# Key masks ahead of the next chunk's decays, map transposes between two halves, and a join whose gaps hold other work

## The reference, cut to what matters

```python
def step(S, inp):
    r_t, w_t, k_t, v_t, a_t, b_t = inp
    sa = jnp.einsum('bhij,bhj->bhi', S, a_t)
    S = S * w_t[:, :, None, :] + sa[..., None] * b_t[:, :, None, :] + v_t[..., None] * k_t[:, :, None, :]
    y = jnp.einsum('bhij,bhj->bhi', S, r_t) if emit else None
    return S, y
```

```python
xn = rms_norm_2(h, attn_norm_g[layer])
proj = xn @ w_in[layer]
```

## Time and profile before

| what | value |
|---|---|
| runs | 1196.22, 1204.70, 1204.64 us; median 1204.64 |
| profiled execution | 1197.72 us (span 1195.9 us) |
| TensorE | 1131.4 us busy (95%), mean granted clock 0.972 |
| VectorE, ScalarE, GpSimd busy | 645.7, 337.4, 112.4 us |
| chain that ended last | PE 75%, DVE 17%, ACT 3%, DMA 2% |

### The profile page before, as it was taken

How to read it: one execution, slowest core, us unless ns; L and a number is a source line. 1 busy time by engine, 2 the same in 40 slices (tenths; PEclk the granted TensorE clock), 3 DMA queues, 4 the chain that set the end, 5 groups by cost and what they waited for, 6 DMA issues and landing times.

```text
span 1195.9 us, 15595 instructions
## 1 busy us (share of the span) xinstructions
PE 1131.4 (95%) x6191; PEld 787.1 (66%) x6191; DVE 645.7 (54%) x1360; ACT 337.4 (28%) x786; POOL 112.4 (9%) x107
## 2 busy tenths in 40 slices
PE   4899999979878999999999999999999999999997
PEld 2444857657778686556478888644555488888543
DVE  3222315766997965798226666631698135665400
ACT  2212223765643224225121121200525112112100
POOL 0000101110120011161000000100360000000000
PEclk9799999998888989999999999999999999999999
DMA  9722342000003202742248443434432354454410
GB/s 356 271 71 78 121 141 76 1 1 1 2 1 100 98 11 71 281 141 71 71 120 277 141 141 141 163 119 142 160 121 71 98 184 141 142 166 173 154 35 35
DMA packets 96666, 140.06 MB, mean 117 GB/s; under 512 B 12207, under 2 KB 63058, under 8 KB 96466
## 3 DMA queue, kind: packets, MB, share of 16 engines
q1 hardware_dynamic: 96228, 138.94, 34.2%
q10 hardware_dynamic: 366, 0.13, 0.0%
HBM read 138.01 MB, written 1.05 MB: 116 GB/s over the span
## 4 chain that ended last, share of the span: by engine, by line
PE 75%; DVE 17%; ACT 3%; DMA 2%; issue 2%; SPq 0%; POOL 0%; DVEq 0%; ACTq 0%
PE bank L1335 25%; PE bank L1354 13%; PE bank L825 12%; PE bank L480 2%; PE bank L473 2%; PE bank L1163 2%; DMA ring<-in_ada_w 2%; DVE work L2594 2%; DVE work L2589 1%; PE bank L1153 1%; PE bank L1044 1%; PE bank L1097 1%; PE bank L619 1%; DVE rot L2574 1%; DVE ring L2159 1%
## 5 line engine op out<-in xcount | busy, mean ns | idle before, releaser
L1335 PE MATMUL bank<-work,ring 128*128 128x256 f32 x1024 | 222.7, 379 | 0.0
L1335 PEld LDWEIGHTS bank<-work,ring 128*128 128x128 f32 x1024 | 194.2, 190 | 26.2
L825 PE MATMUL bank<-work,ring 128*128 128x256 f32 (+1 forms) x432 | 141.0, 485 | 2.4 <-ACT work L1405 2.4
L1354 PE MATMUL bank<-ring,work 128*128 128x512 f32 x288 | 124.2, 592 | 0.0
L825 PEld LDWEIGHTS bank<-work,ring 128*128 128x128 f32 x432 | 82.7, 194 | 56.0 <-issue 49.4
L1853 ACT ACTIVATE work<-work,prm 128x256 f32<-128x256 f32 x88 | 48.0, 593 | 250.5 <-DVE work L2734 224.0
L1354 PEld LDWEIGHTS bank<-ring,work 128*128 128x128 f32 x288 | 54.7, 190 | 68.0 <-issue 67.4
L2726 DVE TENSOR_TENSOR work<-bank,turned 128x512 f32<-128x512 f32 x44 | 30.4, 692 | 112.0 <-PE bank L1335 111.9
L1335 PE MATMUL bank<-work 128*128 128x256 f32 x384 | 83.9, 379 | 0.0
L1335 PEld LDWEIGHTS bank<-work 128*128 128x128 f32 x384 | 73.0, 190 | 9.9
L2744 DVE SCALAR_TENSOR_TENSOR work<-work,prm 128x256 f32<-128x256 f32 x176 | 77.1, 480 | 4.2 <-ACT work L1853 2.6
(11 more groups left out here) (454 smaller groups left out, 1759.7 us busy)
## 6 DMA issues: line engine op xcount, KB each, us to landing
ring<-in_w_up SPq DMA_DIRECT2D x32, 1024.0 KB, 7.7
ring<-in_w_in SPq DMA_DIRECT2D x24, 1024.0 KB, 7.7
ring<-in_w_down SPq DMA_DIRECT2D x16, 1024.0 KB, 6.0
ring<-in_ada_w SPq DMA_DIRECT2D x12, 1024.0 KB, 11.0
work<-in_w_up SPq DMA_DIRECT2D x12, 1024.0 KB, 7.7
ring<-in_w_out SPq DMA_DIRECT2D x10, 1024.0 KB, 6.2
work<-in_w_in SPq DMA_DIRECT2D x4, 1024.0 KB, 8.5
work<-in_w_down SPq DMA_DIRECT2D x4, 1024.0 KB, 6.0
```

Of the source, the lines that this page charges most:

```text
L825: ins = mm(b[0:rows, 0:toks], wt[:, k, off:off + rows], hT[:, k, 0:toks], start=(k == 0), stop=(k == KD - 1))
L1335: ins = mm(b[:, SEQ * half:SEQ * half + SEQ], wt[:, KD * half + k, P * j:P * j + P], xnT[:, k, :], start=(k == 0), stop=(k == KD - 1))
L1354: ins = mm(acc[2 * t + j][:, :], actT[:, k, P * t:P * t + P], wt[:, q, 512 * j:512 * j + 512], start=(k == 0), stop=(k == FB - 1))
```

## The change

The same instructions are issued, none is added or taken out (one semaphore, `row_inv`, is new). Five orders change:

1. `mask_tokens(n)` on VectorE comes ahead of `decayed(n+1)` and `rates(n+1)` in chunks 1 to 3 and 6, and between them in chunk 5. Chunks 4 and 7 stay.
2. In both joins ScalarE spreads the diagonals from the rows' result as soon as that exists (`row_inv`), copies `mid`, and spreads the others behind it.
3. In the second join one of the two bonus banks is filled behind `mid`, the other behind `corner`, and behind that the last matmul of the early projection; ScalarE copies that bank later. VectorE takes the bonus banks before `state_inputs`.
4. In both layers the small maps' transposes stand between `xa` 1 and `xa` 2.
5. ScalarE empties `xa` 0 before the last squares and `xa` 2 ahead of the maps; VectorE empties `xa` 1 before `wsT`.

```diff
@@ tensor: joins, early projection @@
                 ins.then_inc(*filling(("mid", p)))
                 if p:
-                    bonus_sums()
+                    bonus_sums(0)
                 pe.wait_ge(*when_empty(("mid", p)))
...
                 ins.then_inc(*filling(("corner", p)))
+                if p:
+                    bonus_sums(1)
...
-            project_early(0)
+            project_early(0, 0)
+            project_early(0, 1)
             advance(2)
             advance(3)
-            project_early(1)
+            project_early(1, 0)
+            project_early(1, 1, range(3))
+            join_quarters(1)
+            project_early(1, 1, range(3, 4))
             weights_done(("early", 1, 1))
-            join_quarters(1)
@@ tensor: seams @@
-                def to_channels(key, x, ready):
+                def to_channels(key, x, ready, between=None):
                     for j in range(4):
+                        if j == 2 and between:
+                            between()
                         if j % 2 == 0:
                             pe.wait_ge(*ready(j // 2))
...
-                    to_channels("xa", xc, lambda j: when_empty(("down", l - 1, 2 + j)))
+                    to_channels("xa", xc, lambda j: when_empty(("down", l - 1, 2 + j)), small_maps)
@@ scalar: joins @@
             def spread_quarters(p):
-                act.wait_ge(S["t_inv"], p + 1)
-                for d in range(2):
+                def diagonals(d):
+                    act.wait_ge(S[("row_inv", "t_inv")[d]], p + 1)
                     for q in range(2):
...
+                diagonals(0)
                 key = ("mid", p)
...
                 A.activation(mid, b[:, :], ACT.Copy).then_inc(*emptying(key))
+                diagonals(1)
...
             spread_quarters(1)
             state_parameters(0)
+            take_early(1, 1)
@@ scalar: seams @@
                 for t in range(2):
                     cols, q = slice(512 * j, 512 * j + 512), 2 * j + t
+                    if q == 3:
+                        channels_even(0, "xa", "attn_g", 0)
                     act.wait_ge(S["x1"], q + 1)
...
                     for q in range(4):
+                        if q == 2:
+                            channels_even(l, "xa", "attn_g", 0)
                         square_sum(2 * l, q, when_empty(("down", l - 1, 2 * (q % 2) + q // 2)))
+                channels_even(l, "xa", "attn_g", 2)
                 take_maps()
-                channels_even("xa", "attn_g", 0)
-                channels_even("xa", "attn_g", 2)
@@ vector @@
-                step(V.transpose(sq_c.rearrange("p (n x) -> p x n", n=32), t3))
+                V.transpose(sq_c.rearrange("p (n x) -> p x n", n=32), t3).then_inc(S["row_inv"], 1)
+                aside(next(passed))
...
             for n in range(1, 4):
+                mask_tokens(n)
                 decayed(n + 1)
                 rates(n + 1)
-                mask_tokens(n)
                 scaled(n + 1)
...
             for n in range(4, 8):
+                if n == 6:
+                    mask_tokens(n)
                 if n < 7:
                     decayed(n + 1)
+                    if n == 5:
+                        mask_tokens(n)
                     rates(n + 1)
-                mask_tokens(n)
+                if n in (4, 7):
+                    mask_tokens(n)
...
             join(1)
-            state_inputs(0)
             for j in range(2):
                 vec.wait_ge(*when_full(("bonus", j)))
...
+            state_inputs(0)
...
+                channels_odd("xa", "attn_g", (1,))
                 take_mixing()
-                channels_odd("xa", "attn_g")
+                channels_odd("xa", "attn_g", (3,))
```

More of the change, by code:

```diff
@@ L1037, in _, with project_early @@
             wt_a = weights("out_attention", 4, 1024)
-            def project_early(j):
-                for t in range(2):
+            def project_early(j, t, ks=range(4)):
+                if ks[0] == 0:
                     pe.wait_ge(*turn(("early", j, t)))
-                    b = bank_of(("early", j, t))
-                    for k in range(4):
-                        ins = mm(b[:, :], mixT[:, 4 + k, P * t:P * t + P], wt_a[:, k, 512 * j:512 * j + 512], start=(k == 0), stop=(k == 3))
+                b = bank_of(("early", j, t))
+                for k in ks:
+                    ins = mm(b[:, :], mixT[:, 4 + k, P * t:P * t + P], wt_a[:, k, 512 * j:512 * j + 512], start=(k == 0), stop=(k == 3))
+                if ks[-1] == 3:
                     ins.then_inc(*filling(("early", j, t)))
@@ L1687, in state_tables, with channels_even @@
                 A.activation(csc[:, :, 1, :], ang, ACT.Sin, bias=small[:, 383:384], scale=-TWO_PI).then_inc(S["tables"], 1)
+            def channels_even(l, key, gain, j):
+                act.wait_ge(*when_full((key, l, j)))
+                b = bank_of((key, l, j))
+                for i in range(2):
+                    k = 2 * j + i
+                    ins = A.activation(xnT[:, k, :], b[:, SEQ * i:SEQ * i + SEQ], ACT.Copy, scale=k2(l, gain, 1, k))
+                ins.then_inc(*emptying((key, l, j)))
             act.wait_ge(S["mix_rw"], 2)
@@ L2512, in take_scales, with channels_odd @@
                     vec.wait_ge(*when_empty((key, l, "row")))
-                def channels_odd(key, gain):
-                    for j in range(1, 4, 2):
+                def channels_odd(key, gain, js=(1, 3)):
+                    for j in js:
                         vec.wait_ge(*when_full((key, l, j)))
```

79 lines of the change are left out of this document (37 added, 42 removed).

## The result

| | kernel before | changed kernel |
|---|---|---|
| median of the runs, us | 1201.39 (1196.22 to 1204.70, 4 runs) | 1185.57 (1181.88 to 1189.21, 4 runs) |
| ratio, 95% interval | | 0.9878 (0.9850 to 0.9907) |
| profiled execution, us | 1197.72, span 1195.9 | 1189.21, span 1187.4 |
| mean granted clock of it | 0.972 | 0.968 |

The forecast was 1186. The two profiled spans show 8.5 us of the gain where the medians show 15.8: the profiled execution before was 3.7 us faster than its median, and that of the changed kernel, the slowest of its four, 3.6 slower. The stages can be compared by landmarks of the two traces.

What follows compares the result with a forecast made beforehand. TensorE, 75% of the chain, was taken as the bound through its idle time and half clock. Gains 7.0 + 3.2 + 1.7 + 2.8 = 14.7 took 1197.7 to 1183.0; 3.5 for the median gave 1186.5, stated as 1186, range 1176 to 1198.

Steps and rivals of the forecast that it cites:

- Chunks 1 to 3, forecast 7.0: Masking ak before the next chunk's decays removes TensorE's waits there: 7.0 us, bounds 3.0 and 7.5.
- so 5.8 - 0.4 + 1.5 = 6.9: Chunks 1 to 3: 5.8 us idle removed, less 0.4 new wait for rotated queries, plus 1.5 for the clock.
- The term for the clock, 1.5: Chunk 3: work behind the 2.83 us wait ran at a fallen clock; removing the wait saves 1.5 us.
- Chunks 4 to 7, forecast 3.2: First solve 3.2 us earlier, bounds 0 and 6.5; chunk 6's wait moves ahead of line 661 as 5.7 us.
- In chunk 5 [...] the 1.61 go: Chunk 5: with the mask ahead of the rates only, TensorE's 1.61 us wait disappears.
- The path gains 0.8: First join: mid is copied 1.3 us earlier, but VectorE waited only 0.78 us for TensorE, so 0.8 us gained.
- Second join, forecast 1.7: Second join: add_cross starts 1.7 us earlier, bounds 0.5 and 2.2; VectorE's state_steps are late next.
- Seams, forecast 2.8: Layer seams: waits of 1.90 us (layer 0) and 0.95 (layer 1) go, 0.78 stays; 2.8 us, bounds 1.4 and 2.9.
- The first (the gap in chunk 6 only moved): Chunk 6: the gap only moves and the clock stays down; chunks 4 to 7 give nothing, 1189.7 us; chance 0.2.
- The second rival (gains given back): VectorE takes back half of 7.0 and 1.7, chunks 4 to 7 give 0: 1194.1 us against the median; chance 0.17.
- The third: The five waits named after line 2032 end by another release; only seams and join gain: 1196.7 us; chance 0.05.
- The fourth: Slower: VectorE waits for ak(n) ahead of the decays, delaying chunk n+1, plus another half-clock spell: 1212 us; chance 0.04.

Runs made afterwards that it cites:

- e7_late_6: Changed kernel with chunk 6's masks put back behind decays and rates; median 1187.21 us, ratio 0.9886 to the kernel before.
- e2_masks_56: Kernel before with only the masks of chunks 5 and 6 moved; median 1200.57 us, ratio 0.9968.
- e6_fill_6: Changed kernel with keyed_values(6) computed four times into the same bank; median 1184.91 us, ratio 0.9853 to the kernel before.
- e1_masks_13: Kernel before with only the masks of chunks 1 to 3 moved ahead of the next chunk's decays; median 1193.92 us, ratio 0.9914.
- e3_joins: Kernel before with only the joins' part of the change; median 1199.79 us, ratio 0.9970.
- e4_seams: Kernel before with only the seams' part (small maps' place, early emptying of xa banks); median 1196.43 us, ratio 0.9963.
- e5_reads_6: Changed kernel with all four masks of chunk 6 ahead of decayed(7); median 1183.16 us, ratio 0.9843 to the kernel before.
- e8_dense_gap: e5_reads_6 with twelve thrown-away 128x512 matmuls in the gap ahead of nt(7); median 1197.14 us, ratio 0.9952 to the kernel before.
- the gate columns: e5_reads_6 with both groups of gate columns moved from behind the read-outs into them; median 1185.07 us, ratio 0.9864 to the kernel before.
- e11_both: e5_reads_6 with keyed_values(6) computed four times and only gate 0 moved into the read-outs; median 1178.92 us, ratio 0.9819 to the kernel before.

## Why the prediction was right

**Total.** Forecast 14.7 us; the ratio says 14.7 (11.2 to 18.0). The mechanism is right: the waits went where it said, and the new ones came where it said. The exact hit is in part luck. The forecast had 3.2 us for the clock (1.5 in chunk 3, 1.7 in chunk 6) and 11.5 for the rest. Measured are 12.0 to 13.1 us at an equal clock and some 4 for the clock, but the clock's part is an average over executions whose spells the forecast could not know. Two terms are right by parts that lean opposite ways.

**Chunks 1 to 3, forecast 7.0.** The step "so 5.8 - 0.4 + 1.5 = 6.9" held: 6.5 us at the first key head, 7.7 to 8.3 by the end of the attention, 5.0 alone at an equal clock. The three waits went, the new one was 0.72, and VectorE took nothing back. The term for the clock, 1.5, was too small: 7 us less at 1.2 GHz in that stretch, which at 0.44 each is 3. (Between single profiles this varies: 14 to 18 us in the four without the moved masks, 3 to 10 in the ten with them.)

**Chunks 4 to 7, forecast 3.2.** The new wait came in the place named and within 0.2 us of its size (5.7 forecast, 5.89 measured). Without the first join the forecast was 2.4; measured 1.2 to 2.4. Its inner split was wrong: "In chunk 5 [...] the 1.61 go" is no gain of its own, as `e7_late_6` shows, because chunk 6 waits for VectorE and not for TensorE. "The path gains 0.8" at the first join was 0.1 alone and 0.6 together with the masks. That step rests on a misread row: the 0.78 us in the earlier trace rows are the wait of a mask at line 2032 for `rb` (line 619), 3.4 us behind the join. `join` itself, line 2181 at 321.79, waited for nothing.

**Second join, forecast 1.7:** 1.9 by the stretch up to `add_cross`, and what is late next is VectorE's state steps, as said. Alone it gave 0.9.

**Seams, forecast 2.8:** 3.4 by the traces where no spell fell into the seam. Both terms were a little small: 2.2 for 1.90 in layer 0, where the last two banks' transposes also take 1.09 us in place of 1.26, and 1.2 for 0.95 in layer 1.

**Rivals.** The first (the gap in chunk 6 only moved) is true of the idle time: 4.79 became 5.89. Of the gain it is half true. Behind `read_keys(5)` the changed kernel gained 0.2 and 1.0 us on before in its two profiles, and `e2_masks_56` nothing. What chunks 4 to 7 gained besides came from chunk 5, and only `e7_late_6` shows that it needs chunk 6's masks. Of the rule named there, from the Trainium skill, "TensorE: Matmul & The Clock Gate", section "HAM oscillation — how this bites in real kernels": `e6_fill_6` agrees with it in part, since line 661's work ran at full clock once the wait was filled (1.97 us for 3.65). The read-outs do not fit it, where the clock fell with TensorE busy throughout, and neither does the short spell of `e6_fill_6` from 352.3 on. The second rival (gains given back) did not come from VectorE. The third is excluded: each of the five waits went with its mask. The fourth is excluded by the result itself, and for chunks 1 to 3 by `e1_masks_13`.

**What the forecast missed.** It carried the spells of low clock over from the trace of before, and named this as its weakest point. The read-outs lost 7.6 us to them in the first profile and 6.4 in the second, more than any term but one. In the two profiled executions the total did not hold: 8.5 us in place of 14.7, and the read-outs are most of what is missing. It held in the medians, since the other executions of the change had less of the lower clock (0.973 to 0.978 against 0.968 in the profiled one). That was not foreseen, and is luck.

Left open: why the same matmuls of solves and read-outs spend 10 us at the lower clock in some profiles (before, `e3_joins`), 17 to 21 in others (`e1_masks_13`, `e2_masks_56`, `e4_seams`, `e5_reads_6`, `e6_fill_6`), and 27 to 31 in four (both of the change, `e7_late_6`, `e8_dense_gap`). The instructions there are the same; what differs is when they start and what ran ahead. No run here isolated it.

## What to carry to other kernels

When a wait of the bounding engine is named after a helper engine, ask whether that helper has slack at that place. Where it waited itself (chunks 1 to 3), putting its small release ahead of its long work gained the whole wait. Where it is the limit (chunks 5 and 6), the wait moved to the next thing it releases: the first reorder alone gave nothing, and the two in a row 1.2 to 2.4 us. And before moving work into a busy stretch, look at what it was covering where it stood (the gate columns).

## What the runs showed of the hardware that I had not expected

- The granted clock falls to one half in stretches in which TensorE never waits: 29.3 us busy of 30 at 0.51. In all fourteen profiles every spell in the read-outs began during the matmuls of 64 rows with 64 columns (lines 812 and 778 in the changed kernel) or at most 1.4 us behind them. Eight larger matmuls among them went with a clock of 0.95 in place of 0.72 in one profile. That these small matmuls are the cause is not shown.
- A float32 matmul has two records in the timeline: of about 0.45 us each with 512 columns (twelve matmuls, x24), and also with 64 (the 32 of the repeated `keyed_values(6)`, x64). A transpose has one. A price taken from a count in a row must say which it counts.
- Between executions of one kernel the clock goes with most of the scatter: 0.44 us for each us at 1.2 GHz, with 1.5 us left over.
- The spells repeat in a few patterns. Nine profiles with the same instructions ahead of chunk 6 show three, which differ by 7 us at the lower clock and 4 us of time in one stretch of 90 us.
- Four times the work in a gap can be free: 5.4 us of repeated matmuls (`e11_both`) ended where VectorE's release came, and `nt(7)` then waited 0.46 us.
